# Five convolved tiles of the input projection as 512-column products, with VectorE joining the two halves

## The chip, the cores and the metric

The kernel runs on one core of one Trainium2 chip. The metric is the time of one execution on the device, in microseconds; three executions are shown below and their median is what counts. Engines are named as in the profile: PE is TensorE (PEld its weight loads), ACT is ScalarE, DVE is VectorE, SP issues the DMAs.

## The reference

One layer of a streaming encoder over 256 tokens. What matters here is the input projection `proj = rmsnorm(x) @ w_in` and what the second mixer does with 1280 of its columns (`xbc`):

```python
def causal_dwconv(x, w, b):
    k_w = w.shape[0]
    seq = x.shape[1]
    xp = jnp.pad(x, ((0, 0), (k_w - 1, 0), (0, 0)))
    return sum(xp[:, k:k + seq] * w[k] for k in range(k_w)) + b

def mamba2_mixer(p, conv_w, conv_b, dt_bias, a_log, d_skip, norm_g):
    ...
    xbc = jax.nn.silu(causal_dwconv(xbc, conv_w, conv_b))
    xs, b_in, c_in = jnp.split(xbc, [SSM_INNER, SSM_INNER + SSM_GROUPS * SSM_STATE], axis=-1)
```

All inputs are 32-bit floats.

## The kernel before

**Split products.** Each 32-bit matrix is used as two parts, `hi` (rounded to the format that PE multiplies fast) and `lo` (the rest). A product is the sum of three: hi·hi, hi·lo and lo·hi. Weights arrive as 1 MB tiles, numbered n through the whole kernel: SP loads tile n into `raw[n % 3]`, ACT casts it to `hi` (L400), DVE subtracts to get `lo` (L829), PE multiplies. The ring is three tiles deep (`RING = 3`), so SP may load tile n + 3 only after DVE has made `lo` of tile n. In round n of the loops ACT and DVE split tile n + 2.

**Two ways to multiply a tile of w_in.** A tile is 2048 x 128 weights; the activations have 256 tokens, and their two parts lie side by side in `ux` (`uh` and `ul` are its halves). `tile_product` (narrow) issues three 256-column matmuls for each of the 16 k-blocks, 48 in all (L1436, L1437, L1438), which add up all three products in the first 256 columns of a PSUM bank; it needs `lo` from the start. `wide_product` issues 16 matmuls of 512 columns with `hi` (L1461), which leave hi·uh in columns 0 to 255 and hi·ul in 256 to 511, and then 16 of 256 columns with `lo` (L1467) onto the first half. It needs `lo` only for its last third, but somebody has to add the halves. Tiles 8 to 13 and 25 to 33 are done wide: ACT copies the second half out (`take_low`, L517) and DVE adds the first (`sum_halves`, L958). Product banks go round by n % 3.

**The ten convolved tiles** are n = 15 to 24 (N_XBC = 15, N_QKV = 25), all narrow. In round n, ACT casts tile n + 2, waits for product n, then (`conv_first`) writes tap 0 with the bias to `convacc` (L590) and a copy of the product to `convraw` (L592), whose signal `tile_taken` also frees the bank; then it waits for DVE's `conv_done` of tile n - 1 and applies SiLU (L597, signal `xbc_ready`). DVE in round n makes `lo` of tile n + 2, does some small work that belongs to that round (the dt rows of the scan, variances, reciprocals, rotations), and then `conv_rest`: three taps, each a scalar_tensor_tensor that waits for the one before (L1055). `go` is the helper for an instruction after which DVE waits for its completion. Most buffers in SBUF appear in the profile under the one name `arena`.

**What follows.** Before tile 26 PE issues a few small matmuls (L1723, L1724) that need `xbc_ready` of all ten tiles. From round 27 on it spreads the decays of two heads of the scan each round (L1735, L1736), and for heads 2 and 3 it waits on `seg_ready`, which DVE signals at L1149 in its own round 27. Order is fixed by each engine's instruction list; nothing is scheduled at run time.

Of the kernel before, what the change touches and what calls it, by code (L numbers as in the profile page):

```python
# [17 lines left out]
ALU, ACT, AX = mybir.AluOpType, mybir.ActivationFunctionType, mybir.AxisListType  # L18

P = 128  # L20
T = 256
# [8 lines left out]
RING = 3  # L30
# [11 lines left out]
N_XK, N_XV, N_CQ, N_KRDT, N_XBC, N_QKV, N_ZA, N_U, N_ZB, N_OUT, N_WQ, N_WO, N_FFN = 0, 4, 8, 14, 15, 25, 31, 34, 38, 41, 57, 61, 65  # L42
# [6 lines left out]
V_CW = V_ROWS_A  # L49
# [42 lines left out]
def products(n):  # L92

    extra = {N_U: 3, N_U + 1: 3, N_U + 2: 6, N_U + 3: 1}
    return n + 1 + sum(v for m, v in extra.items() if m <= n)
# [25 lines left out]
def encoder(nc, x, mem, positions, norm_mix, w_in, mla_q_norm, mla_w_uq, mla_kv_norm, mla_w_ukv, mla_out_norm,  # L121
# [4 lines left out]
    with ctx:  # L126
        def sb(name, shape, dt=F32):
            return ctx.enter_context(nc.sbuf_tensor(name, shape, dt))
# [3 lines left out]
        def S(name):  # L132

            if name not in signals:
                signals[name] = Signal(ctx.enter_context(nc.semaphore(name)))
            return signals[name]
# [9 lines left out]
        vecs = sb("vecs", [P, V_ALL])  # L146
        small = sb("small", [P, 112])
        arena = sb("arena", [P, 20400])
        bank = [ctx.enter_context(nc.psum_tensor(f"bank{i}", [P, 512], F32)) for i in range(8)]
# [3 lines left out]
        def at(off, *shape):  # L153

            size = int(np.prod(shape))
            v = arena[:, off:off + size]
            if len(shape) == 2:
                v = v.rearrange("p (a b) -> p a b", b=shape[1])
            if len(shape) == 3:
                v = v.rearrange("p (a b c) -> p a b c", b=shape[1], c=shape[2])  # L160
            return v
# [9 lines left out]
        convraw, convacc = at(4096, RING, T), at(4864, RING, T)  # L171
# [219 lines left out]
        def _(act):  # L391
            a = Engine(act)
# [112 lines left out]
            def wait_product(n):  # L505
                act.wait_ge(S("products_done").sem, products(n))
# [71 lines left out]
            a.mark(act.copy(krT[64:128, :], b[0:64, 0:T]), S("kr_parts"))  # L578
            a.mark(act.copy(dt_rows[0:SSM_H, 0, :], b[64:64 + SSM_H, 0:T]), S("tile_taken"))
            act.wait_ge(S("tile_summed").sem, summed(N_CQ + 5))  # L580
            squares("cq", cq_raw[:, 0:4, :], sq_cq, 4)
            squares("ckv", cq_raw[:, 4:6, :], sq_ckv, 2)

            def conv_first(n):

                c = n - N_XBC
                wait_product(n)
                if c >= RING:
                    act.wait_ge(S("xbc_ready").sem, c - RING + 1)
                a.mark(act.activation(convacc[:, n % RING, :], bank[n % 3][:, 0:T], ACT.Identity,  # L590
                                      scale=vecs[:, V_CW + 30 + c:V_CW + 31 + c], bias=vecs[:, V_CB + c:V_CB + c + 1]), S("conv_first"))
                a.mark(act.copy(convraw[:, n % RING, :], bank[n % 3][:, 0:T]), S("tile_taken"))  # L592

            def conv_silu(n):
                c = n - N_XBC
# [218 lines left out]
        def _(dve):  # L814
# [3 lines left out]
            def go(ins, signal=None):  # L818
                d.mark(ins, signal or step)
                d.settle()  # L820
# [227 lines left out]
            def conv_rest(n):  # L1048

                c = n - N_XBC  # L1050
                dve.wait_ge(S("tile_taken").sem, TAKEN_XBC + c + 1)
                s = n % RING
                for k in (1, 2, 3):
                    col = V_CW + 10 * (3 - k) + c
                    go(dve.scalar_tensor_tensor(out=convacc[:, s, k:T], in0=convraw[:, s, 0:T - k], scalar=vecs[:, col:col + 1],  # L1055
                                                in1=convacc[:, s, k:T], op0=ALU.mult, op1=ALU.add),
                       S("conv_done") if k == 3 else None)

            def rotate(tile):

                for q in range(4):
                    d.mark(dve.tensor_copy(rot[32 * q:32 * q + 32, :], tile[32 * (q ^ 1):32 * (q ^ 1) + 32, :]), step)
                d.settle()
                go(dve.tensor_tensor(rot, rot, sinT, ALU.mult))
                go(dve.tensor_tensor(tile, tile, cosT, ALU.mult))
                go(dve.tensor_tensor(tile, tile, rot, ALU.add), S("rotated"))
# [5 lines left out]
            for n in range(N_XBC, N_XBC + 10):  # L1072
# [49 lines left out]
                if n == 23:  # L1122
                    feature_scale("cq", cq_raw[:, 0:4, :], 4, rtmp_a)
                conv_rest(n)
                if n == 24:
                    feature_scale("ckv", cq_raw[:, 4:6, :], 2, rtmp_b)
# [46 lines left out]
            for n in range(N_SSD, N_OUT + 1):  # L1173
# [27 lines left out]
                if N_U + 2 <= n <= N_ZB:  # L1201
                    k = n - N_U - 2
                    dve.wait_ge(S("tile_taken").sem, TAKEN_U + 7 + k)
                    rotate(qr[:, k, :])
# [218 lines left out]
        def _(pe):  # L1423
            done = S("products_done").sem

            def ready(n, i=None, per=0):

                pe.wait_ge(S("lo_ready").sem, n + 1 if i is None else i * per + n + 1)
# [11 lines left out]
            def tile_product(n, b, cols=P, mid=None, lo_signal=None, ks=(0, KD)):  # L1440

                s = n % RING
                for k in range(*ks):
                    if k == KD // 2 and mid:
                        mid()
                    if lo_signal and k % 2 == 0:
                        pe.wait_ge(S(lo_signal).sem, k + 2)
                    last = three(bank[b][0:cols, 0:T], hi[:, s, k * P:k * P + cols], lo[:, s, k * P:k * P + cols],
                                 uh[:, k, :], ul[:, k, :], k == 0, k == KD - 1)
                if ks[1] == KD:  # L1450
                    last.then_inc(done, 1)

            def wide_product(n, b, ks=(0, KD), i=None, mid=None, lo_signal=None):

                s = n % RING
                turn = 0 if i is None else i * GROUP
                pe.wait_ge(S("hi_ready").sem, turn + n + 1)
                for k in range(*ks):
                    if lo_signal and k % 2 == 0:
                        pe.wait_ge(S(lo_signal).sem, k + 2)  # L1460
                    pe.matmul(bank[b][:, :], hi[:, s, k * P:(k + 1) * P], ux[:, k, :, :].rearrange("p a b -> p (a b)"),  # L1461
                              start=(k == 0), stop=False)
                if mid:
                    mid()
                pe.wait_ge(S("lo_ready").sem, turn + n + 1)
                for k in range(*ks):
                    last = pe.matmul(bank[b][:, 0:T], lo[:, s, k * P:(k + 1) * P], uh[:, k, :], start=False, stop=(k == KD - 1))  # L1467
                if ks[1] == KD:
                    last.then_inc(done, 1)
# [116 lines left out]
            def both(f, pair):  # L1586
                f(2 * pair)
                f(2 * pair + 1)
# [93 lines left out]
            tile_product(N_KRDT, N_KRDT % 3, ROPE + SSM_H)  # L1682

            def w_in_tile(n, mid=None):
                if N_KRDT <= n - 3 < N_QKV:
                    pe.wait_ge(S("tile_taken").sem, TAKEN_XBC + n - 3 - N_KRDT)
                else:
                    pe.wait_ge(S("tile_summed").sem, summed(n - 3))
                if n < N_QKV:
                    ready(n)  # L1690
                    tile_product(n, n % 3, mid=mid)
                else:
                    wide_product(n, n % 3, mid=mid)
# [58 lines left out]
            def latent_tile(index, w0, wcols, k0, kn_, s):  # L1752
                if index < 3:
                    pe.wait_ge(S("tile_summed").sem, summed(N_ZA + index))
                else:
                    pe.wait_ge(S("tile_taken").sem, TAKEN_U + index - 2)
                b = bank[(products(N_U - 1) + index) % 3]
# [15 lines left out]
            for n in range(N_SSD, N_OUT):  # L1773
                s = n % RING
# [57 lines left out]
                else:  # L1832
                    pe.wait_ge(S("tile_taken").sem, TAKEN_U + 15 + (n - N_ZB) - 2)
                    wide_product(n, z_bank(n), mid=mid)
# [25 lines left out]
            for cb in range(4):  # L1860
                n = N_OUT + cb
# [6 lines left out]
            for cb in range(4):  # L1868
                n = N_OUT + 4 + 3 * cb
# [28 lines left out]
            for n in (N_WQ + 2, N_WQ + 3):  # L1898
                ready(n)

                def mid():
                    if n == N_WQ + 2:
                        pe.wait_ge(S("tile_taken").sem, TAKEN_U + 17)
                        both(scores, A_X // 2)
# [3 lines left out]
            both(head_out, A_X // 2)  # L1908
            pe.wait_ge(S("tile_taken").sem, TAKEN_U + 19)
            both(scores, A_X // 2 + 1)  # L1910
# [101 lines left out]
OUT_CHUNKS = [(3, cb) for cb in range(4)] + [(g, cb) for cb in range(4) for g in range(3)]  # L2012
N_VECTORS = 16 * (9 + 1 + 3 + 1)
TAKEN_XBC = 1
TAKEN_U = TAKEN_XBC + 10
N_SSD = 27
N_PAIR = 33


def summed(n):  # L2020

    return n - N_CQ + 1 - (11 if n > N_KRDT else 0) - (4 if n >= N_ZB else 0)


def z_bank(n):
    return n % 3 if n < N_U else (n - N_ZB + 1) % 3
# [58 lines left out]
```

## Time and profile before

| | us |
|---|---|
| median of 3 executions | 1180.62 |
| lowest, highest | 1179.78, 1180.98 |
| the profiled execution, whole | 1180.57 |
| its span, first to last instruction | 1178.4 |
| PE busy in it | 1165.5 (99%) |
| DVE busy | 898.6 (76%) |
| ACT busy | 660.3 (56%) |
| mean granted TensorE clock | 0.999 |

The w_in tiles begin at about 61 us; the feed-forward layer runs from about 450 us to the end. Times in the rows are microseconds from the span's start. "Busy" counts the time covered by an instruction's record, and consecutive matmuls overlap in the records, so the time of a tile is read from the start of its first matmul to the start of the next tile's first.

### The profile page before, as it was taken

The numbers are of one execution on the slowest core, as the hardware profiler recorded it, in microseconds if no ns is written. First come the engines' busy times: TensorE is split into PE (matmuls) and PEld (weight loads), VectorE is DVE, ScalarE is ACT, GpSimd is POOL, SyncE is SP. The second block draws the span as 40 slices with busy tenths as digits, with TensorE's granted clock in tenths as the row PEclk, the third lists the DMA queues.
The fourth block names the chain that finished last, engine by engine and source line by source line (L and its number), as shares of the span: only waits on it lengthen the run. The fifth ranks groups of instructions, "written<-read, shape, count | busy, mean of one in ns | idle before, by whom it ended". The sixth has DMA issues, their size and how long they took to land.

```text
span 1178.4 us, 18270 instructions
## 1 busy us (share of the span) xinstructions
PE 1165.5 (99%) x6666; PEld 1022.8 (87%) x6666; DVE 898.6 (76%) x1286; ACT 660.3 (56%) x872; POOL 3.0 (0%) x5
## 2 busy tenths in 40 slices
PE   8999999999999999999999999999999999999997
PEld 8889998898888988888888888888888888888885
DVE  6885998887966677777777776777777776777777
ACT  6646664566645567455555545455555545455455
POOL 0000000000000000000000000000000000000000
PEclk9999999999999999999999999999999999999999
DMA  9967646543666546675757566575757566575751
GB/s 346 261 153 191 180 129 164 154 119 110 223 205 183 195 127 175 181 212 179 214 178 203 179 190 191 164 213 178 214 178 202 179 192 187 166 213 178 214 179 71
DMA packets 303628, 217.00 MB, mean 184 GB/s; under 512 B 11383, under 2 KB 264543, under 8 KB 302943
## 3 DMA queue, kind: packets, MB, share of 16 engines
q1 hardware_dynamic: 303262, 215.91, 62.9%
q8 instruction: 30, 0.49, 0.2%
q10 hardware_dynamic: 320, 0.47, 0.1%
q14 instruction: 16, 0.12, 0.0%
HBM read 214.27 MB, written 2.10 MB: 184 GB/s over the span
## 4 chain that ended last, share of the span: by engine, by line
PE 92%; DVE 5%; issue 1%; ACT 1%; DMA 0%; DVEq 0%; ACTq 0%
PE bank L1461 32%; PE bank L1467 17%; PE bank L1433 10%; PE bank L1435 10%; PE bank L1434 10%; PE bank L1436 2%; PE bank L1614 2%; PE bank L1437 2%; PE bank L1438 2%; DVE lo L829 1%; PE bank L1552 1%; PE bank L1583 1%; DVE arena L1055 1%; PE bank L1490 1%; PE bank L1497 1%
## 5 line engine op out<-in xcount | busy, mean ns | idle before, releaser
L829 DVE TENSOR_TENSOR lo<-raw,hi 128x2048 fp32r<-128x2048 f32 x195 | 446.0, 2288 | 112.8 <-ACT hi L400 104.7
L400 ACT CAST hi<-raw 128x2048 fp32r<-128x2048 f32 x194 | 370.5, 1915 | 95.9 <-PE bank L1435 95.6
L1461 PE MATMUL bank<-ux,hi 128*128 128x512 f32 x1696 | 406.2, 391 | 0.0
L1461 PEld LDWEIGHTS bank<-ux,hi 128*128 128x128 f32 x1696 | 312.3, 188 | 61.2 <-DVE arena L1360 0.2
L1467 PEld LDWEIGHTS bank<-ux,lo 128*128 128x128 f32 x1696 | 217.2, 191 | 8.9 <-issue 1.0
L1467 PE MATMUL bank<-ux,lo 128*128 128x256 f32 x1696 | 221.2, 283 | 0.0
L1433 PE MATMUL bank<-hi,ch 128*128 128x512 f32 x462 | 180.7, 391 | 0.0
L1434 PE MATMUL bank<-lo,ch 128*128 128x512 f32 x462 | 179.5, 389 | 0.0
L1435 PE MATMUL bank<-hi,cl 128*128 128x512 f32 x462 | 179.5, 388 | 0.0
L783 ACT COPY arena<-bank 128x256 f32<-128x256 f32 x88 | 32.9, 374 | 195.1 <-PE bank L1467 195.0
L1339 DVE SCALAR_TENSOR_TENSOR arena<-arena,vecs 128x255 f32<-128x255 f32 (+1 forms) x176 | 85.0, 483 | 24.4 <-DVE arena L1339 3.6
L1435 PEld LDWEIGHTS bank<-hi,cl 128*128 128x128 f32 x462 | 86.7, 188 | 18.1
L1433 PEld LDWEIGHTS bank<-hi,ch 128*128 128x128 f32 x462 | 86.8, 188 | 17.5 <-issue 0.2
L1434 PEld LDWEIGHTS bank<-lo,ch 128*128 128x128 f32 x462 | 86.8, 188 | 17.2
L1359 DVE TENSOR_TENSOR arena<-bank,arena 128x256 f32<-128x256 f32 x88 | 37.1, 422 | 55.3 <-ACT arena L783 55.3
L1436 PE MATMUL bank<-ux,hi 128*128 128x256 f32 (+1 forms) x240 | 68.6, 286 | 0.0
L1438 PE MATMUL bank<-ux,lo 128*128 128x256 f32 (+1 forms) x240 | 67.8, 283 | 0.0
L1437 PE MATMUL bank<-ux,hi 128*128 128x256 f32 (+1 forms) x240 | 67.8, 283 | 0.0
L1272 DVE TENSOR_TENSOR arena<-arena,bank 128x512 f32<-128x512 f32 x96 | 60.9, 680 | 3.6 <-PE bank L1435 3.5
L771 ACT ACTIVATE arena<-arena,vecs 128x256 f32<-128x256 f32 x88 | 53.4, 607 | 17.2 <-DVE arena L1360 17.1
L1437 PEld LDWEIGHTS bank<-ux,hi 128*128 128x128 f32 (+1 forms) x240 | 45.3, 189 | 0.1
L1436 PEld LDWEIGHTS bank<-ux,hi 128*128 128x128 f32 (+1 forms) x240 | 45.3, 189 | 0.1
(274 smaller groups left out, 1014.9 us busy)
## 6 DMA issues: line engine op xcount, KB each, us to landing
raw<-in_ffn_w_up_dram SPq DMA_DIRECT2D x88, 1024.0 KB, 5.8
raw<-in_ffn_w_down_dram SPq DMA_DIRECT2D x44, 1024.0 KB, 5.1
raw<-in_w_in_dram SPq DMA_DIRECT2D x28, 1024.0 KB, 5.6
raw<-in_w_out_dram SPq DMA_DIRECT2D x16, 1024.0 KB, 5.3
raw<-in_cross_wkv_dram SPq DMA_DIRECT2D x7, 1024.0 KB, 10.0
arena<-in_x_dram SPq DMA_DIRECT2D x4, 1024.0 KB, 8.6
raw<-in_cross_wq_dram SPq DMA_DIRECT2D x4, 1024.0 KB, 5.5
raw<-in_cross_wo_dram SPq DMA_DIRECT2D x4, 1024.0 KB, 5.3
```

The costliest lines, as they stand in the source:

```text
L400: a.mark(act.copy(hi[:, n % RING, :], raw[:, n % RING, :]), S("hi_ready"))
L829: d.mark(dve.tensor_tensor(lo[:, n % RING, :], raw[:, n % RING, :], hi[:, n % RING, :].bitcast(F32), ALU.subtract), S("lo_ready"))
L1272: d.mark(dve.tensor_tensor(hres[:, t, cb * 512:(cb + 1) * 512], hres[:, t, cb * 512:(cb + 1) * 512], bank[b][:, :], ALU.add), signal)
L1339: go(dve.scalar_tensor_tensor(out=cacc[:, s, tap:T], in0=craw[:, s, 0:T - tap], scalar=vecs[:, bass.ds(col, 1)], in1=cacc[:, s, tap:T], op ...
L1433: pe.matmul(dst, xh, wh, start=start, stop=False)
L1434: pe.matmul(dst, xh, wl, start=False, stop=False)
L1435: return pe.matmul(dst, xl, wh, start=False, stop=stop)
L1436: pe.matmul(dst, wh, xh, start=start, stop=False)
L1437: pe.matmul(dst, wh, xl, start=False, stop=False)
L1438: return pe.matmul(dst, wl, xh, start=False, stop=stop)
L1461: pe.matmul(bank[b][:, :], hi[:, s, k * P:(k + 1) * P], ux[:, k, :, :].rearrange("p a b -> p (a b)"), start=(k == 0), stop=False)
L1467: last = pe.matmul(bank[b][:, 0:T], lo[:, s, k * P:(k + 1) * P], uh[:, k, :], start=False, stop=(k == KD - 1))
```

## The change

Tiles 15 to 19 (N_NARROW = N_XBC + 5 = 20) go through `wide_product` instead of `tile_product`. For them ACT's tap 0 takes columns 0 to 255 as before, and its copy takes columns 256 to 511. DVE gets two instructions ahead of its three taps: a scalar_tensor_tensor that adds tap 0 of the second half from PSUM to `convacc`, and a tensor_tensor that adds the first half from PSUM to the copy in `convraw`; the latter signals `tile_summed` and frees the bank. The counts of the signals follow.

```diff
@@ ACT, conv_first
-                a.mark(act.copy(convraw[:, n % RING, :], bank[n % 3][:, 0:T]), S("tile_taken"))
+                if n < N_NARROW:
+                    a.mark(act.copy(convraw[:, n % RING, :], bank[n % 3][:, T:2 * T]), S("low_taken"))
+                else:
+                    a.mark(act.copy(convraw[:, n % RING, :], bank[n % 3][:, 0:T]), S("tile_taken"))
@@ DVE, conv_rest
-                dve.wait_ge(S("tile_taken").sem, TAKEN_XBC + c + 1)
                 s = n % RING
+                if n < N_NARROW:
+                    dve.wait_ge(S("low_taken").sem, summed(n))
+                    go(dve.scalar_tensor_tensor(out=convacc[:, s, :], in0=bank[n % 3][:, T:2 * T], scalar=vecs[:, V_CW + 30 + c:V_CW + 31 + c],
+                                                in1=convacc[:, s, :], op0=ALU.mult, op1=ALU.add))
+                    go(dve.tensor_tensor(convraw[:, s, :], bank[n % 3][:, 0:T], convraw[:, s, :], ALU.add), S("tile_summed"))
+                else:
+                    dve.wait_ge(S("tile_taken").sem, TAKEN_XBC + n - N_NARROW + 1)
@@ PE, w_in_tile
-                if N_KRDT <= n - 3 < N_QKV:
-                    pe.wait_ge(S("tile_taken").sem, TAKEN_XBC + n - 3 - N_KRDT)
+                if n - 3 == N_KRDT:
+                    pe.wait_ge(S("tile_taken").sem, TAKEN_XBC)
+                elif N_NARROW <= n - 3 < N_QKV:
+                    pe.wait_ge(S("tile_taken").sem, TAKEN_XBC + n - 3 - N_NARROW + 1)
                 else:
                     pe.wait_ge(S("tile_summed").sem, summed(n - 3))
-                if n < N_QKV:
+                if N_NARROW <= n < N_QKV:
                     ready(n)
                     tile_product(n, n % 3, mid=mid)
@@ constants
+N_NARROW = N_XBC + 5
-TAKEN_U = TAKEN_XBC + 10
+TAKEN_U = TAKEN_XBC + N_QKV - N_NARROW
-    return n - N_CQ + 1 - (11 if n > N_KRDT else 0) - (4 if n >= N_ZB else 0)
+    return n - N_CQ + 1 - (1 if n > N_KRDT else 0) - (N_QKV - N_NARROW if n >= N_QKV else 0) - (4 if n >= N_ZB else 0)
```

In the lists below `arena` is SBUF (here `convacc` and `convraw`), `bank0` a PSUM bank, `vecs` the per-feature scalars, and the words after "waits" are the signals. DVE in round 15, before: the last two of the small instructions on the dt rows, the three taps of tile 15, and `lo` of tile 18.

```order
L1078 TENSOR_TENSOR arena<-arena 12x256 [waits vector_step]
L1079 TENSOR_SCALAR arena<-arena 12x256 [waits dt_abs]
L1055 SCALAR_TENSOR_TENSOR arena<-arena,vecs 128x255 [waits tile_taken,vector_step]
L1055 SCALAR_TENSOR_TENSOR arena<-arena,vecs 128x254 [waits vector_step]
L1055 SCALAR_TENSOR_TENSOR arena<-arena,vecs 128x253 [waits vector_step]
L829 TENSOR_TENSOR lo<-raw,hi 128x2048 [waits products_done,hi_ready,conv_done]
```

DVE at the same place in the changed kernel (its lines L1085 to L1088 are the old L1076 to L1079, L1064 is the old L1055, L832 the old L829):

```order
L1087 TENSOR_TENSOR arena<-arena 12x256 [waits vector_step]
L1088 TENSOR_SCALAR arena<-arena 12x256 [waits dt_abs]
L1057 SCALAR_TENSOR_TENSOR arena<-bank0,vecs,arena 128x256 [waits low_taken,vector_step]
L1059 TENSOR_TENSOR arena<-bank0,arena 128x256 [waits vector_step]
L1064 SCALAR_TENSOR_TENSOR arena<-arena,vecs 128x255 [waits tile_summed]
L1064 SCALAR_TENSOR_TENSOR arena<-arena,vecs 128x254 [waits vector_step]
L1064 SCALAR_TENSOR_TENSOR arena<-arena,vecs 128x253 [waits vector_step]
L832 TENSOR_TENSOR lo<-raw,hi 128x2048 [waits products_done,hi_ready,conv_done]
```

Two instructions stand ahead of the taps, each followed by a wait for its completion, and `lo` of tile 18 now stands behind five instead of three. The same is so in rounds 16 to 19.

PE from the end of tile 14 (76 columns of weights) into tile 15, before:

```order
L1437 MATMUL bank<-ux,hi 76x256
L1438 MATMUL bank<-ux,lo 76x256
L1436 MATMUL bank<-ux,hi 128x256 [waits lo_ready,tile_summed]
L1437 MATMUL bank<-ux,hi 128x256
L1438 MATMUL bank<-ux,lo 128x256
```

The same place in the changed kernel, with the whole of tile 15 and the first matmul of tile 16:

```order
L1446 MATMUL bank<-ux,hi 76x256
L1447 MATMUL bank<-ux,lo 76x256
L1470 MATMUL bank<-ux,hi 128x512 [waits hi_ready,tile_summed]
L1470 MATMUL bank<-ux,hi 128x512 x15
L1476 MATMUL bank<-ux,lo 128x256 [waits lo_ready]
L1476 MATMUL bank<-ux,lo 128x256 x15
L1470 MATMUL bank<-ux,hi 128x512 [waits hi_ready,tile_summed]
```

The three kinds of 256-column matmuls, 16 of each, have become 16 of 512 and 16 of 256 columns, and `lo` is waited for two thirds of a tile later.

## Rows read from the trace of the kernel before

**Rows 1.** The page: busy time of each engine, and DMA issues of w_in.

```profile
PE 1165.5 (99%) x6666; PEld 1022.8 (87%) x6666; DVE 898.6 (76%) x1286; ACT 660.3 (56%) x872; POOL 3.0 (0%) x5
...
raw<-in_w_in_dram SPq DMA_DIRECT2D x28, 1024.0 KB, 5.6
```

**Rows 2.** PE timeline: start us, us, engine, line, operation; first matmuls of tiles.

```profile
66.72 3.82 PE L1461 MATMUL bank<-ux,hi 128*128 128x512 f32 x16
...
72.29 3.82 PE L1461 MATMUL bank<-ux,hi 128*128 128x512 f32 x16
...
100.16 0.28 PE L1436 MATMUL bank<-ux,hi 128*128 128x256 f32 x1
...
105.91 0.28 PE L1436 MATMUL bank<-ux,hi 128*128 128x256 f32 x1
...
128.95 0.28 PE L1436 MATMUL bank<-ux,hi 128*128 128x256 f32 x1
```

**Rows 3.** DVE timeline in rounds 16 to 19; in brackets idle before, and releaser.

```profile
116.33 2.29 DVE L829 TENSOR_TENSOR lo<-raw,hi 128x2048 fp32r<-128x2048 f32 x1 [0.84 <-ACT hi L400]
...
123.25 2.29 DVE L829 TENSOR_TENSOR lo<-raw,hi 128x2048 fp32r<-128x2048 f32 x1
...
127.84 2.29 DVE L829 TENSOR_TENSOR lo<-raw,hi 128x2048 fp32r<-128x2048 f32 x1 [0.86 <-ACT hi L400]
...
130.04 0.41 DVE L1092 TENSOR_TENSOR arena<-arena 12x256 f32<-12x256 f32 x1
```

**Rows 4.** Windows, DVE alone: stretch, its length, DVE busy (instructions), clock, DMA.

```profile
127.90:179.50 51.60, 48.97 (x81) 1.00 0.60 159
```

**Rows 5.** The chain that ended last, from 123 to 181 us: start, length, what.

```profile
131.83 0.50 DVE arena L1055
132.35 0.49 DVE arena L1055
...
176.40 2.15 issue
180.24 0.38 PE bank L1735
```

**Rows 6.** Durations (min/median/max ns) by line, and DVE's timeline at 455 us.

```profile
L1164 DVE SCALAR_TENSOR_TENSOR arena<-arena,small,bank x6: 472/474/480, 189.4 to 223.1; 128x256 f32<-128x256 f32 x6
...
L958 DVE TENSOR_TENSOR arena<-bank,arena x18: 408/418/426, 67.6 to 288.5; 128x256 f32<-128x256 f32 x18
...
455.88 0.42 DVE L1359 TENSOR_TENSOR arena<-bank,arena 128x256 f32<-128x256 f32 x1
456.33 0.42 DVE L1360 TENSOR_TENSOR arena<-arena 128x256 f32<-128x256 f32 x1
```

**Rows 7.** Timeline of all engines around the two places where PE meets DVE's work.

```profile
165.49 0.42 ACT L597 ACTIVATE arena<-arena 128x256 f32<-128x256 f32 x1 [0.23 <-DVE arena L1055]
...
166.05 0.67 PE L1723 MATMUL bank<-arena 128*128 128x256 f32 x2
...
179.47 0.38 PE L1735 MATMUL bank<-acum_h,pick 128*128 128x256 f32 x1 [0.25 <-DVE arena L1149]
...
180.24 0.38 PE L1735 MATMUL bank<-acum_h,pick 128*128 128x256 f32 x1 [0.27 <-DVE arena L1149]
```

**Rows 8.** Waits of PE from 180 to 1170 us: total, times, longest.

```profile
PE bank L1562 <- issue: 0.7, 1, 0.7
PE bank L1735 <- DVE arena L1149: 0.3, 1, 0.3
```

**Rows 9.** PE's last matmul, and windows (length, PE busy, clock, DMA) behind it.

```profile
1169.61 0.39 PE L1435 MATMUL bank<-ux,cl 128*128 128x512 f32 x1
...
1174.00:1175.00 1.00, 0.00 (x0) 0.94 0.16 64
1175.00:1176.00 1.00, 0.00 (x0) 0.50 1.03 402
```

**Rows 10.** Waits of all engines from 90 to 200 us: total, times, longest.

```profile
ACT arena L590 <- PE bank L1438: 15.2, 9, 3.7
```

## The prediction, made before the changed kernel ran

> **What bounds the kernel now.** I read the page's busy times first: PE is busy for 99% of the span, DVE for 76% [rows 1], so at first sight only PE's own work counts, and a cheaper tile would be a gain. Then I asked PE's waits from 180 us to its end: two or three, about 1 us in all [rows 8]. So whatever PE loses before 180 us is not won back later, and whatever it gains before a wait is only worth something if the wait ends earlier too.
>
> The stretch that the change touches is 100 to 180 us, and there the chain of waits tells another story than the shares. From about 128 us on it runs through DVE and not through PE, one instruction behind the other, to the head spread at 180.24, which PE waits for [rows 5]. The reader should see two things. First, DVE is full: of the 51.6 us from 127.9 to 179.5 it is busy for 48.97, over 81 instructions [rows 4], and the 2.6 us that are left are the hand-over times of some 0.03 us between dependent instructions, not waits on another engine. Second, PE meets this chain at two places. At 166.05 it starts the small products that need all ten convolved tiles; the SiLU of the last one ran from 165.49 to 165.91, after a 0.23 us wait for DVE's taps [rows 7]. PE arrives there at the very moment when its operand is ready. At 179.47 and 180.24 it is already late, 0.25 and 0.27 us by the records, waiting for DVE's L1149 [rows 7]. So PE is full, and DVE is full behind it with no reserve: the two run neck and neck.
>
> **The change part by part.**
>
> PE's work. A wide tile takes 72.29 - 66.72 = 5.57 us, a narrow one 105.91 - 100.16 = 5.75 us [rows 2]. Five tiles at 0.18 make 0.9 us less of PE. This is the whole gain that the change can have.
>
> ACT's work. The same two instructions per tile with another address: nothing. ACT waits for PE 15.2 us in nine waits before tap 0 [rows 10], so its longer waits for `conv_done` have cover. I followed the one that could hurt: the SiLU of tile n - 1 stands ahead of the cast of tile n + 2. In round 18 the taps of tile 17 end at 125.3 (below), the SiLU and the cast of tile 21 take 0.4 and 1.9 us, and DVE needs that cast at 130.0. It is there 2.3 us earlier. If this cover went, DVE would be late by the difference.
>
> DVE's work. Two instructions more in each of five rounds. The scalar_tensor_tensor with a PSUM operand is L1164, 474 ns; the tensor_tensor is L958, 418 ns [rows 6]. Both are followed by a wait for completion. The taps show what that adds: 0.49 us each, but 132.35 - 131.83 = 0.52 from start to start [rows 5]; the PSUM add at 455.88 has a dependent instruction 0.45 behind it [rows 6]. So 0.51 + 0.45 = 0.96 us per round, 4.8 us in all. The bounds: if the hand-over were as short as the overlap that independent instructions get (`lo` at 127.84 lasts 2.29 us and the next instruction starts at 130.04 [rows 3], 0.09 before its end), 0.71 to 0.8 per round, 3.6 to 4.0 in all; above, nothing in the trace is dearer than the taps' 0.52, twice 0.52 makes 5.2.
>
> A rule against the rows: DVE's two PSUM rows are no dearer than their SBUF relatives (418 ns for L958 beside 0.42 us for L1360, which has no PSUM operand) [rows 6]. The Trainium skill, "VectorE: DVE Perf Modes", section on the TRN2 errata, has a fixed cost of 120 cycles for a PSUM source and 58 for SBUF at 0.96 GHz, some 65 ns more for each; by it ten instructions would cost 0.65 us more and the time would be 1184.3. The rows disagree, and I go by them.
>
> What of DVE's 4.8 us lies beside idle time. Between the first added instruction at about 109 us and the meeting at 179.5, DVE waits for another engine just twice: 0.84 us before 116.33 and 0.86 before 127.84, both for ACT's cast [rows 3]. After them it is gapless [rows 4]. Both are used up: by the first DVE is 1.9 us behind its old times, by the second 2.0 (1.9 - 0.84 + 0.96, and the fourth round's 0.96 on top). So DVE's delay is +1.0 in round 15, +1.9 in 16, less 0.84, +2.0 after 17, +3.0 after 18, less 0.86, +3.1 after 19, and stays there: 4.8 - 1.7 = 3.1 us.
>
> Who waits for that. (a) `lo` of tile 20, the first narrow one, which PE needs from its start: 123.25 + 2.0 + 2.2 = 127.5; PE comes to tile 20 at 128.95 - 0.9 = 128.0 [rows 2, 3]. It holds by 0.5 us; if it didn't, PE's wait would be covered by what follows. (b) Banks: the first half is now freed by DVE, not ACT, at the latest some 4 us before PE wants it for tile n + 3. (c) Loads: SP waits for `lo` to reload a raw buffer, a load lands after 5.6 us [rows 1] and ACT casts it about a round later than that; it is delayed alike with everything behind DVE, and at its tightest (tile 23, `lo` of tile 20 at 127.5, landed at 133.1, cast not before PE has done tile 20 at 133.8) it is in time. (d) The SiLU of tile 24: 165.49 + 3.1 = 168.6, so the small products at 169.1 instead of 166.05. (e) The spread of heads 2 and 3: 179.47 + 3.1.
>
> The sum. PE arrives at (d) at 166.05 - 0.9 = 165.1 and stands idle for 4.0 us, until 169.1. Its gain of 0.9 is swallowed there. The following 13 us of PE's work are the same as before, and at (e) DVE is again the later one, by 3.1. From there both go on as before, PE without waits that could absorb anything [rows 8]. The change is +3.1 us on the profiled execution of 1180.57, which is 0.05 below the median: **1183.7 us**, 0.26% slower.
>
> **The rivals.**
>
> *PE sets the end and the gain arrives.* The shares speak for it (99% against 76%), and that PE before 166 has no waits. Then the change is -0.9 and the time 1179.7, not slower. It is one mechanism at one place: the small products at 166.05. It decides this way if the ten added instructions delay the last SiLU by no more than what DVE's idle time swallows, 1.7 us, thus under 0.35 us per round instead of 0.96. Against it is the length of each of the two, 418 and 474 ns.
>
> *Cheap hand-overs.* At 0.8 us per round the delay is 4.0 - 1.7 = 2.3 us, the time 1182.9; at 0.71 it is 1182.4. For it: some DVE pairs overlap. Against it: both new instructions have a wait behind them in the list.
>
> *The clock falls in PE's new idle time.* At the end of this trace PE's last matmul ends at 1170.0, and the granted clock goes from full to half at about 1174.9 (0.94 in that microsecond, 0.50 after) [rows 9], 4.9 us after PE stopped; the new pause is 4.0 us long. If it fell there, PE would start again at half speed. For a spell as long as the pause it would lose 2.0 us, of which about 0.4 are covered before the wait at (e), since PE arrives there early by that much: +1.6, 1185.3. The Trainium skill, "TensorE: Matmul & The Clock Gate", advises against idle gaps of PE about this long and would put the clock at 1.2 GHz for a while; the end of this trace agrees that it falls, though only after a longer stop.
>
> *The change does not do what it says* (a tile still goes narrow, or PE waits for `lo` at the start of a wide one): the order shows 16 and 16 matmuls with `lo_ready` in the middle, so I give it nothing.
>
> **How the numbers follow.** My forecast (DVE's delay of about 3.1) 0.77, with 1183.0 to 1184.4 as its own range; the clock 0.11; cheap hand-overs 0.07; the gain arrives 0.05. A measurement of this kernel can tell about 0.2% from no change, 2.4 us, so slower means above 1183.0. Forecast and clock are above, the two others below it; some of the forecast's lower edge may fall under, so slower 0.84, same 0.15, faster 0.01 (it would need 1178.2, more than the whole gain). The range takes in cheap hand-overs and the clock: 1182.4 to 1185.4.
>
> **What would show it.** Right: tiles 15 to 19 at 5.57 us from start to start; DVE's two new lines at about 0.47 and 0.42, and no wait for ACT's cast left between 110 and 175; one pause of PE of about 4 us before the small products, released by the SiLU; the wait for L1149 at about 182.6 as short as before; everything after at +3.1. Wrong: PE pausing earlier (tile 20), or ACT's cast still keeping DVE waiting, which would mean a longer way through ACT; a wide tile in this place slower than 5.57; a pause much shorter than 4 us, which would mean that DVE had reserve that the rows don't show; a granted clock under 1.00 behind the pause.

## The result: 1183.5 us, 2.8 slower than before

| | before | changed |
|---|---|---|
| median of 9 executions, us | 1180.66 | 1183.48 |
| lowest, highest | 1179.65, 1181.47 | 1183.03, 1184.92 |
| ratio, 95% interval | | 1.0029 (1.0019 to 1.0038) |
| span of the profiled execution | 1178.4 | 1181.6 |
| DVE busy | 898.6 | 903.5 |
| mean granted TensorE clock | 0.999 | 0.996 |

The forecast was 1183.7, in a range of 1182.4 to 1185.4. The page of the changed kernel: PE is busy as long as before and DVE 4.9 us longer [rows 1]; in the chain that ended last, DVE's share has gone up to 7% (from 5%).

```profile
PE 1165.8 (99%) x6586; PEld 1020.0 (86%) x6586; DVE 903.5 (76%) x1296; ACT 658.9 (56%) x872; POOL 3.0 (0%) x5
...
PE 91%; DVE 7%; issue 1%; ACT 1%; DMA 0%; DVEq 0%; ACTq 0%
```

PE's timeline (start, length, line, operation, and in brackets idle time and releaser) answers to [rows 2] and [rows 7]. L1470 and L1476 are the old L1461 and L1467, L1734 the small products (L1723), L1746 the spreads (L1735):

```profile
105.36 3.82 PE L1470 MATMUL bank<-ux,hi 128*128 128x512 f32 x16
...
110.92 3.82 PE L1470 MATMUL bank<-ux,hi 128*128 128x512 f32 x16
...
162.79 2.07 PE L1476 MATMUL bank<-ux,lo 128*128 128x256 f32 x16
168.93 1.19 PE L1734 MATMUL bank<-arena 128*128 128x256 f32 x2 [4.06 <-ACT arena L600]
...
171.48 4.11 PE L1470 MATMUL bank<-ux,hi 128*128 128x512 f32 x16
...
183.37 0.28 PE L1746 MATMUL bank<-acum_h,pick 128*128 128x256 f32 x1
```

The wide tiles take 110.92 - 105.36 = 5.56 us. PE is done with tile 25 at 164.9 and stands idle for 4.06 us, until ACT's SiLU (L600, the old L597) has the last convolved tile. DVE's timeline answers to [rows 3] and [rows 6]; L832 is `lo`, L1064 the taps:

```profile
108.42 0.48 DVE L1057 SCALAR_TENSOR_TENSOR arena<-bank,vecs,arena 128x256 f32<-128x256 f32 x1
108.94 0.42 DVE L1059 TENSOR_TENSOR arena<-bank,arena 128x256 f32<-128x256 f32 x1
109.40 1.52 DVE L1064 SCALAR_TENSOR_TENSOR arena<-arena,vecs 128x255 f32<-128x255 f32 x3
110.95 2.29 DVE L832 TENSOR_TENSOR lo<-raw,hi 128x2048 fp32r<-128x2048 f32 x1
...
117.08 2.29 DVE L832 TENSOR_TENSOR lo<-raw,hi 128x2048 fp32r<-128x2048 f32 x1
...
129.73 2.29 DVE L832 TENSOR_TENSOR lo<-raw,hi 128x2048 fp32r<-128x2048 f32 x1
```

The pair takes 109.40 - 108.42 = 0.98 us, and the two brackets of [rows 3], 0.84 and 0.86 us of waiting for ACT's cast, are gone at 117.08 and 129.73.

**How executions are compared below.** PE's start of tile 14, before anything that was changed, lies anywhere from 94.17 (this profile) over 94.56 (before) to 95.99 us in the profiled executions. So places in the traces are given from that start: the small products ("first meeting") and the start of tile 28, behind the spread of heads 2 and 3 ("second meeting").

| | tile 14 at | small products, from there | tile 28, from there | median, us | its before | ratio (95%) |
|---|---|---|---|---|---|---|
| before | 94.56 | 71.49 | 86.02 | 1180.66 | | |
| changed | 94.17 | +3.27 | +3.64 | 1183.48 | 1180.66 | 1.0029 (1.0019 to 1.0038) |
| no_adds | 94.56 | -0.74 | -0.73 | 1179.70 | 1180.44 | 0.9992 (0.9983 to 1.0001) |
| load_only | 95.12 | +3.27 | +3.72 | 1184.10 | 1180.44 | 1.0027 (1.0017 to 1.0036) |
| load_in_gap | 95.11 | +0.01 | +0.02 | 1179.84 | 1180.44 | 0.9996 (0.9987 to 1.0005) |
| pe_kept_busy | 95.79 | +3.26 | +3.28 | 1183.20 | 1180.44 | 1.0023 (1.0014 to 1.0032) |
| two_wide | 95.03 | +0.32 | +0.32 | 1180.77 | 1180.38 | 1.0001 (0.9992 to 1.0011) |
| gap_filled_0 | 94.55 | -0.02 | -1.17 | 1179.37 | 1180.38 | 0.9990 (0.9981 to 1.0000) |
| gap_filled_2 | 95.39 | -0.38 | -1.53 | 1179.32 | 1180.71 | 0.9987 (0.9978 to 0.9996) |
| gap_filled_3 | 95.99 | -0.57 | -1.72 | 1178.38 | 1180.71 | 0.9982 (0.9973 to 0.9991) |
| gap_filled_4 | 95.19 | -0.26 | -1.13 | 1179.99 | 1180.38 | 0.9996 (0.9987 to 1.0005) |
| gap_filled_5 | 95.74 | +0.68 | -0.18 | 1179.92 | 1180.38 | 0.9998 (0.9989 to 1.0007) |
| ten_wide | 94.57 | +8.15 | +9.11 | 1189.24 | 1180.71 | 1.0073 (1.0059 to 1.0086) |

### The profile page after: what moved, and what is told of

Same layout as the page of the kernel before. It is cut to its first block, busy times and chain, and to the rows that moved or that the text cites. A ratio compares the mean times of both kernels' runs of the same rounds, so it can differ in the third digit from the quotient of the medians.

```text
span 1181.6 us, 18120 instructions
## 1 busy us (share of the span) xinstructions
PE 1165.8 (99%) x6586; PEld 1020.0 (86%) x6586; DVE 903.5 (76%) x1296; ACT 658.9 (56%) x872; POOL 3.0 (0%) x5
## 4 chain that ended last, share of the span: by engine, by line
PE 91%; DVE 7%; issue 1%; ACT 1%; DMA 0%; DVEq 0%; ACTq 0%
PE bank L1470 32%; PE bank L1476 17%; PE bank L1442 10%; PE bank L1443 10%; PE bank L1444 10%; PE bank L1623 2%; DVE lo L832 2%; PE bank L1445 1%; PE bank L1446 1%; PE bank L1447 1%; DVE arena L1064 1%; PE bank L1561 1%; PE bank L1592 1%; PE bank L1499 1%; PE bank L1506 1%
## 5 line engine op out<-in xcount | busy, mean ns | idle before, releaser
L832 DVE TENSOR_TENSOR lo<-raw,hi 128x2048 fp32r<-128x2048 f32 x195 | 446.1, 2288 | 110.0 <-ACT hi L400 101.8
L1470 PE MATMUL bank<-ux,hi 128*128 128x512 f32 x1776 | 425.4, 391 | 0.0
L1470 PEld LDWEIGHTS bank<-ux,hi 128*128 128x128 f32 x1776 | 327.2, 188 | 64.1 <-DVE arena L1369 0.2
L1476 PEld LDWEIGHTS bank<-ux,lo 128*128 128x128 f32 x1776 | 227.5, 191 | 9.3 <-issue 1.0
L1476 PE MATMUL bank<-ux,lo 128*128 128x256 f32 x1776 | 231.6, 283 | 0.0
L1445 PE MATMUL bank<-ux,hi 128*128 128x256 f32 (+1 forms) x160 | 46.0, 287 | 0.0
L1446 PE MATMUL bank<-ux,hi 128*128 128x256 f32 (+1 forms) x160 | 45.2, 282 | 0.0
L1447 PE MATMUL bank<-ux,lo 128*128 128x256 f32 (+1 forms) x160 | 45.2, 282 | 0.0
L1369 DVE TENSOR_TENSOR arena<-arena 128x256 f32<-128x256 f32 x88 | 37.4, 426 | 3.0
L882 DVE SCALAR_TENSOR_TENSOR ux<-bank,vecs,ux 128x256 fp32r<-128x256 f32 x64 | 26.6, 476 | 14.6 <-ACT ux L456 14.6
```

The costliest lines, as they stand in the source:

```text
L832: d.mark(dve.tensor_tensor(lo[:, n % RING, :], raw[:, n % RING, :], hi[:, n % RING, :].bitcast(F32), ALU.subtract), S("lo_ready"))
L1445: pe.matmul(dst, wh, xh, start=start, stop=False)
L1446: pe.matmul(dst, wh, xl, start=False, stop=False)
L1447: return pe.matmul(dst, wl, xh, start=False, stop=stop)
```

## The experiments

Theory A is the forecast's: DVE's queue says when PE may go on at both meetings. Theory B: PE's own work sets the end. Theory C: the wide form itself costs, in ACT or in the banks.

### DVE's load without the wide products, and the wide products without DVE's load

load_only: the kernel before, with

```diff
@@ conv_rest, all ten tiles narrow
+                if n < N_XBC + 5:
+                    go(dve.scalar_tensor_tensor(out=dec[:, 0, 0:T], in0=bank[5][:, T:2 * T], scalar=vecs[:, V_CW + 30:V_CW + 31],
+                                                in1=convacc[:, s, :], op0=ALU.mult, op1=ALU.add))
+                    go(dve.tensor_tensor(dec[:, 1, 0:T], bank[5][:, 0:T], convraw[:, s, :], ALU.add))
```

> The kernel before (all ten tiles narrow), with two DVE instructions of the same size and kind added ahead of the taps in rounds 15 to 19; they read an idle PSUM bank and write to an unused place, so the result is untouched. Theory A: DVE is late by 5 x 0.98 - 1.64 = 3.3 us at the small products and at the head spread; PE, which has no cheaper tiles, waits 2.9 us there instead of 4.0. The end moves by about 3.2, 1183.5 to 1183.9, although no product has changed. Theory C: 1180.7.

```profile
169.88 1.19 PE L1738 MATMUL bank<-arena 128*128 128x256 f32 x2 [3.12 <-ACT arena L600]
...
172.43 4.18 PE L1474 MATMUL bank<-ux,hi 128*128 128x512 f32 x16
```

That is PE's timeline at the small products. They start 169.88 - 95.12 = 74.76 us behind tile 14; in the changed kernel it is 168.93 - 94.17 = 74.76. With narrow tiles and ten DVE instructions whose results nobody reads, PE resumes at the same hundredth, only from a pause of 3.12 instead of 4.06 us (2.9 was expected). So the delay is DVE's load and nothing else, and the cheaper products don't shorten it at all: they lengthen the pause. Theory C is out. The median, 1184.10, is 0.2 above the range that was expected, much less than the width of its interval (2.0 to 4.2 us over the kernel before).

no_adds: the changed kernel with

```diff
@@ conv_rest
-                    go(dve.scalar_tensor_tensor(out=convacc[:, s, :], in0=bank[n % 3][:, T:2 * T], scalar=vecs[:, V_CW + 30 + c:V_CW + 31 + c],
-                                                in1=convacc[:, s, :], op0=ALU.mult, op1=ALU.add))
-                    go(dve.tensor_tensor(convraw[:, s, :], bank[n % 3][:, 0:T], convraw[:, s, :], ALU.add), S("tile_summed"))
...
-                       S("conv_done") if k == 3 else None)
+                       S("conv_done") if k == 3 else S("tile_summed") if k == 1 and n < N_NARROW else None)
```

> The changed kernel, with DVE's two new instructions left out: the second half's share of tap 0 and the first half of the product are missing from the five tiles; everything else, the wide products too, stays. Theory A (DVE's queue sets when PE may go on at both meeting points): DVE is back at its old times, PE reaches the small products 0.9 us early and waits for the same SiLU as before, so the time is that of the kernel before, 1180.7. Theory B (PE sets the end, the gain of the products is real and only the adds hide it): 0.9 us less, 1179.8. Theory C (the loss is made by the wide form itself: the hand-over of banks, ACT's copy): 1183.5 as changed.

Here theory A as I had put it missed and B had the number: 0.74 us less at both meetings, and 0.74 in the medians (the interval just includes no change). Two lines of DVE's timeline tell why:

```profile
115.95 2.29 DVE L832 TENSOR_TENSOR lo<-raw,hi 128x2048 fp32r<-128x2048 f32 x1 [0.47 <-ACT hi L400]
...
127.09 2.29 DVE L832 TENSOR_TENSOR lo<-raw,hi 128x2048 fp32r<-128x2048 f32 x1 [0.48 <-ACT hi L400]
```

In [rows 3] these stand at 116.33 and 127.84, with 0.84 and 0.86 of waiting. What DVE waits for is ACT's cast, which is queued behind ACT's waits for PE's products. When PE's tiles get shorter the casts come earlier and DVE with them, by 0.38 and 0.75. DVE's old times were not its own: up to 127.84 PE set them, through ACT; behind that DVE runs on its own and carries the lead of 0.75 to both meetings. So PE's gain does reach the end once nothing is added to DVE, 0.74 of the 0.9. The other 0.2 is a short wait of PE at the first meeting: the `lo` part of tile 25 starts 0.94 us earlier than before (163.18 against 164.12), and the small products 2.13 us behind it, where 1.91 pass when PE waits for nothing (gap_filled_3 below). In that much theory A holds: DVE still says when PE may go on.

### The same load where DVE is idle

load_in_gap: ten such instructions, in a row behind `split(N_KRDT + 2)`, ahead of the 5.9 us in which DVE waits for the cast of tile 17.

> The kernel before, with the same ten DVE instructions, all of them placed where DVE sits idle for 5.9 us ahead of the lo part of tile 17. Theory A: 4.9 us of work in a gap of 5.9, so nothing moves, 1180.7. If added DVE work costs wherever it stands (ports, contention with PE or ACT): toward 1183.5.

DVE's wait ahead of `lo` of tile 17, in the kernel before and in this run:

```profile
105.15 2.29 DVE L829 TENSOR_TENSOR lo<-raw,hi 128x2048 fp32r<-128x2048 f32 x1 [5.89 <-ACT hi L400]
```

```profile
105.75 2.29 DVE L832 TENSOR_TENSOR lo<-raw,hi 128x2048 fp32r<-128x2048 f32 x1 [1.16 <-ACT hi L400]
```

The ten instructions have filled the gap (5.89 us of waiting have become 1.16), and counted from tile 14 `lo` of tile 17 starts where it did (10.64 us behind it instead of 10.59). Nothing moved: +0.01 and +0.02 in the trace, and the median 0.6 below its before, inside the interval. The instructions are harmless here; in the full stretch they are not.

### Two tiles, ten tiles

two_wide and ten_wide are the changed kernel with `N_NARROW = N_XBC + 2` and `N_XBC + 10`.

> The change for tiles 15 and 16 only. Theory A: two rounds add 1.96 us to DVE, its two idle stretches swallow 1.64, so DVE is 0.3 late: 1181.0. If the cost goes by the number of wide tiles: two fifths of 2.8, 1181.8. If PE's gain counted: 1180.3.

> The change carried on to all ten convolved tiles, nothing moved. Theory A: in rounds 20 to 24 DVE has no idle time at all, so each further wide tile costs its full 0.98 us; 3.27 + 4.9 = 8.2 us of delay at the small products, 1188.6, and up to 1 more for the clock, which falls in PE's longer pause. If each wide tile costs alike (2.8 / 5 = 0.57): 1186.2.

Two tiles cost 0.32 at both meetings (expected 0.3), ten cost 8.15 at the first (expected 8.2). Per tile that is 0.16 and 0.82: the price of a wide tile depends on how much idle time is left for it. The whole curve is one line, 0.98 a round less 1.63 us. The 1.63 was taken from the five tiles (3.27); two and ten, for which the line gives 0.33 and 8.17, are its test. At the second meeting the ten cost 9.11: there the clock adds 0.96 (next section). The medians (+0.39 and +8.5) agree within their intervals.

### The clock in the pause

Windows of PE in the changed kernel (stretch, length, busy and instructions, granted clock, DMA share, GB/s):

```profile
167.00:168.00 1.00, 0.00 (x0) 1.00 0.00 0
168.00:169.00 1.00, 0.07 (x1) 0.76 0.66 148
169.00:170.00 1.00, 1.00 (x3) 0.50 1.14 345
171.00:172.00 1.00, 1.00 (x4) 0.53 1.10 264
172.00:173.00 1.00, 1.00 (x6) 1.00 0.00 1
```

The clock goes to half at 168.5, just before PE resumes, and comes back at 171.95. The small products take 2.55 us (168.93 to 171.48) where they took 1.30 before, and tile 26 with its two spreads 6.32 instead of 6.13: 1.44 us lost at the lower level. pe_kept_busy fills the pause:

```diff
@@ PE, n == 26, ahead of the wait for xbc_ready
+                    for _ in range(14):
+                        pe.matmul(bank[7][:, :], ux[:, 0, 0, 0:P], ux[:, 0, :, :].rearrange("p a b -> p (a b)"), start=True, stop=True)
```

> The changed kernel, with 14 more 512-column matmuls (3.2 us) on data that is there, into a bank that the next product overwrites, in PE's 4.06 us pause before the small products. The granted clock should stay at 1.00 where it fell to 0.50 from 168.5 to 172.0. Theory: the fall cost what is left after PE's reserve at the next meeting, 0.4 us in the typical run and 1.5 in the two that took 1184.7 and 1184.9; so 1183.1, with no run over 1183.9. Rival: the fall costs all that the slower instructions show, 1.4 us, 1182.1. Rival: it costs nothing, 1183.5.

```profile
170.54 0.67 PE L1736 MATMUL bank<-arena 128*128 128x256 f32 x2 [0.86 <-ACT arena L600]
...
183.97 0.38 PE L1748 MATMUL bank<-acum_h,pick 128*128 128x256 f32 x1 [0.28 <-DVE arena L1158]
...
184.74 0.39 PE L1748 MATMUL bank<-acum_h,pick 128*128 128x256 f32 x1 [0.27 <-DVE arena L1158]
```

The granted clock stays at 1.00 through the pause. The small products start at the same place (+3.26), now at full speed, and PE is early enough at the second meeting to wait for DVE's L1158 (the old L1149) again, with the same two brackets as in [rows 7]. Tile 28 comes at +3.28 instead of +3.64: the fall cost 0.36 us in the profiled execution, the 1.44 less some 1.1 that PE would have waited anyway. That reserve can be read by itself: from the start of tile 27's `lo` part to tile 28 the kernel before takes 180.58 - 177.14 = 3.44 us, the changed one 183.83 - 181.46 = 2.37, so it was 1.07. It holds for the other two falls too: in load_only 1.51 us are lost and the second meeting is 0.45 later than the first, in ten_wide 2.02 and 0.96, so 1.06 are hidden in each. The medians (1183.20 against 1183.48, from different comparisons) are too close to show it. The second half of the expectation missed: three executions still took 1184.6 to 1184.7, at a clock of 0.998 or 0.999. One of them is the profiled one, whose tile 14 starts 1.6 us later than the changed kernel's. At least that one is late from its beginning, not from the clock.

### DVE's other work moved into the gap

gap_filled_k: k tiles wide, and ahead of `split` of tile 17

```diff
+            for wide_ in (pick, acum_h, acum_l):
+                d.mark(dve.memset(wide_[:, :].bitcast(F32), 0.0), step)
+            d.mark(dve.memset(krT_odd[0:64, :], 0.0), step)
+            for g in range(2):
+                d.mark(dve.memset(swa_key[g][0][64:128, :], 0.0), step)
+            dve.wait_ge(S("tile_taken").sem, TAKEN_XBC)
+            go(dve.tensor_scalar(r0, r0, row12[:, 0:1], None, ALU.add))
...
+            sum_tiles("cq", sq_cq, 4, sum_cq)
+            sum_tiles("ckv", sq_ckv, 2, sum_ckv)
```

with the same lines taken out of rounds 15, 16, 21, 22 and 24, and with them a wait for completion behind the three in round 21.

> All ten tiles narrow, as before, but 4.5 us of DVE's small work is moved up into its 5.9 us gap ahead of the lo part of tile 17: the clearing of three small buffers and of three halves of key buffers, the four instructions on the dt rows, and the sums of squares. Theory A: DVE is early enough at the small products (where PE waits for nothing now) and at the head spread, where PE lost 1.07 us before; so 1179.6. Theory B (PE alone sets the end): 1180.7.

With no wide tile the first meeting is where it was and the second 1.17 us earlier: PE's old stall there is gone (expected 1.07). So the moved work is worth 1.17 us by itself, without any cheaper product. The median, 1179.37 (expected 1179.6), has an interval that just reaches no change.

> The change as it was made (tiles 15 to 19 wide), with the same work moved into the gap. Theory A: DVE's delay at the small products is 3.3 - 3.8 = -0.6 us, PE would come 0.9 early, so it waits 0.3 or so; at the head spread some 0.7; the time is 1179.4, 4 us below the changed kernel although every instruction of the change is there. Theory C (the wide form itself): 1183.5 less 1.07.

> The same moves, and tiles 15 to 18 wide. DVE gets 3.9 us of adds and has 1.6 us of waits plus 3.8 to 4.5 us of moved work to set against them, so PE's 0.72 us of cheaper tiles should arrive on top of the 1.07: 1178.9. If any other limit stands close behind DVE (ACT's casts): 1179.6 or more.

Both came out short of the expectation: 1179.92 and 1179.99, and in the traces -0.18 and -1.13 instead of -1.3 and -1.8. DVE's timeline of gap_filled_0 shows the error:

```profile
105.14 2.29 DVE L832 TENSOR_TENSOR lo<-raw,hi 128x2048 fp32r<-128x2048 f32 x1 [0.67 <-ACT hi L400]
...
112.72 1.52 DVE L1064 SCALAR_TENSOR_TENSOR arena<-arena,vecs 128x255 f32<-128x255 f32 x3 [1.54 <-ACT arena L595]
116.31 2.29 DVE L832 TENSOR_TENSOR lo<-raw,hi 128x2048 fp32r<-128x2048 f32 x1 [2.06 <-ACT hi L400]
...
127.83 2.29 DVE L832 TENSOR_TENSOR lo<-raw,hi 128x2048 fp32r<-128x2048 f32 x1 [0.87 <-ACT hi L400]
```

The 2.8 us taken out of rounds 15 and 16 have turned into waits of 1.54 and 2.06 in round 16, and `lo` of tile 21 starts at 127.83 as it did at 127.84. Work moved ahead of a wait is worth no more than the wait lets through: rounds 15 and 16 can take their two adds (1.96 us) for nothing, rounds 17 and 18 have 0.87 against their 1.96, round 19 has nothing. The sum was redone from this. With the 1.0 us cleared out of rounds 21 and 22, and casts that come some 0.4 earlier by round 18, five wide tiles give DVE 1.09 + 0.98 - 1.0 - 0.4 = +0.7 at the first meeting (trace +0.68), and four give -0.3 (trace -0.26), where PE alone would be at -0.9 and -0.7. This was worked out with the results of those two runs at hand; its test is the next two, by which three wide tiles should fit:

> DVE's small work moved into its gap, and tiles 15 to 17 wide. With four wide tiles PE still waited 0.34 us at the small products and about 0.3 at the head spread; one round less takes 0.98 us off DVE and 0.18 off PE's gain. So no wait at either place, and all of 3 x 0.18 + 1.07 = 1.6 us: 1178.8. If the DVE queue is not the reason of those waits, the time falls by the lost gain only: 1180.0.

> The same with tiles 15 and 16 wide: 2 x 0.18 + 1.07 = 1.4 us, 1179.0. Together with 0, 3, 4 and 5 wide tiles it shows where the best number lies: theory A has it at 3.

```profile
166.91 0.59 PE L1731 MATMUL bank<-arena 128*128 128x256 f32 x2
...
179.82 0.28 PE L1743 MATMUL bank<-acum_h,pick 128*128 128x256 f32 x1
...
180.29 2.01 PE L1467 MATMUL bank<-ux,hi 128*128 128x512 f32 x8
```

In gap_filled_3 PE waits at neither meeting: no bracket at the small products (L1731) nor at the spread (L1743). It is at -0.57 and -1.72, the full 3 x 0.18 + 1.17, of which the three wide tiles make 0.55 and the moved work the rest. Its median, 1178.38 us, is the lowest of all, with a ratio of 0.9982 (0.9973 to 0.9991) to the kernel before. Two wide tiles give 1179.32 and 0.9987 (0.9978 to 0.9996), an interval that excludes no change as well. In the traces three are 0.19 us better than two, as expected; the intervals of the medians are too wide to tell the two apart.

## Why the prediction was right, and where it was off

**What bounds it: right.** That DVE is full from 127.9 on and that PE meets it at two places [rows 4, 5, 7] decided the sign. load_only showed it.

**PE's gain of 0.9: right in size, and as forecast it never arrived.** From tile 14 to tile 20 PE takes 127.62 - 94.17 = 33.45 us where it took 128.95 - 94.56 = 34.39: 0.94 less.

**DVE's load: 0.96 us per round forecast, 0.98 measured.** The new lines in the changed kernel, from 106 to 180 us (group, count, busy us, mean ns):

```profile
L1064 DVE SCALAR_TENSOR_TENSOR arena<-arena,vecs 128x255 f32<-128x255 f32 (+2 forms) x30 | 14.5, 483 | 1.0
L1057 DVE SCALAR_TENSOR_TENSOR arena<-bank,vecs,arena 128x256 f32<-128x256 f32 x5 | 2.4, 481 | 0.1
L1059 DVE TENSOR_TENSOR arena<-bank,arena 128x256 f32<-128x256 f32 x5 | 2.1, 424 | 0.2
```

L1057 took 481 ns, not the 474 of L1164, and each pair has the hand-over of the taps. The one that reads PSUM is no dearer than the taps from SBUF (481 beside 483). The Trainium skill ("VectorE: DVE Perf Modes", section on the TRN2 errata) would have it some 65 ns dearer, an estimate from its 120 and 58 cycles at 0.96 GHz; by these rows it is not so here.

**Idle time swallowed: 1.70 forecast, 1.63 measured** (5 x 0.98 - 3.27). DVE's delay at the first meeting: 3.1 forecast, 3.27 in the trace.

**The time: nearer than the mechanism, by luck.** "Everything after at +3.1" was the forecast; counted from tile 14 it is +3.64 at the second meeting and still +3.61 at PE's last matmul (1172.83, before 1169.61). The sum was short by 0.17 of DVE's load and by 0.36 of the clock. The median moved by only 2.8, with an interval of 2.2 to 4.5 us from the ratio, which holds both numbers. That it lies 0.2 from the forecast and not 0.6 comes from parts of the execution that the change doesn't touch, as far as the profiled one shows: its tile 14 began 0.39 us earlier than in the kernel before.

**Waits behind it: right.** No wait of PE before the small products (`lo` of tile 20 held), none of DVE on ACT in the covered part; the pause was 4.06 us where 4.0 was forecast, and its releaser the SiLU. One sign did not show: the wait for the old L1149 at the second meeting was to stay as short as before, and it is gone, since PE came there late after the fall of the clock.

**The rival "PE sets the end" was priced wrongly.** Its point of decision was put at 1.7 us of added work in all. no_adds shows what I had overlooked: the two waits that swallow the load are themselves waits for PE, by way of ACT. The gain pulls their ends forward, and with nothing added 0.74 of it arrives. For the change itself this made no difference, since five adds overrun both waits.

**The clock: wrong.** The likeliest case held that it stays, with 0.11 for the fall, and named a granted clock under 1.00 behind the pause as a sign against itself. It fell, in the profiled execution and, by their mean clocks of 0.995 or 0.996, in eight of the nine (the ninth has 0.997, which some executions without a long pause have too). What kept the forecast near was the cover: 1.44 us lost at the lower level, of which the second meeting hid some 1.1. I had put the loss at 2.0, with a spell at half speed as long as the pause, for which no row spoke: PE worked at the lower level for 3.0 us and lost about half of that. And I had put the reserve at 0.4, where the two waits of [rows 7] together came to 1.07. The rival's +1.6 was therefore too dear: it is 0.36.

## What to carry to other kernels

An engine at 99% is not alone in deciding if another one is full over the stretch at hand: read the busy time per stretch, and follow the chain to the places where the two meet. Saving 0.18 us on the one for 0.98 us on the other pays only where the second has idle time that nothing downstream needs, and that idle time has a place: work put ahead of a wait is free up to the wait's length and gains nothing beyond it. Before adding to an engine's queue, move what can be moved out of it; here that, with three wide tiles for five, turned a loss of 3.6 us in the trace into a gain of 1.7 (2.8 and 2.3 by the medians), of which the moving alone gives 1.17.

## What the runs showed of the hardware

The granted clock went to half in pauses of PE shorter than the 4.9 us at the end of the trace of before [rows 9]: at 168.5 in the changed kernel, 3.6 us after PE's last matmul, and at 169.6 in load_only, 2.8 us after it, in a pause of 3.12 us:

```profile
168.00:169.00 1.00, 0.00 (x0) 1.00 0.00 0
169.00:170.00 1.00, 0.12 (x1) 0.79 0.81 143
```

In both a transfer begins in the same microsecond (the DMA share goes from 0.00 to 0.66 and 0.81), so one might suspect it. In ten_wide the clock falls 3.5 us after the last matmul, in a pause of 9.51 us, with no transfer under way:

```profile
168.00:169.00 1.00, 0.00 (x0) 0.58 0.00 0
```

It stayed at full in the profiled pauses of 1.48 us (gap_filled_5) and 0.86 us (pe_kept_busy). In load_only seven of ten executions have a mean clock of 0.995 or 0.996, one has 0.997, and two have 0.998 and 0.999, as executions without a long pause have; so by the means it fell in some and not in others, with a pause of about 3 us. The Trainium skill ("TensorE: Matmul & The Clock Gate", section on HAM oscillation) warns of idle gaps of PE about this long; the traces agree, and load_only's 3.12 us is a little shorter than the gap that section names. The half level is the lower of the clock's two, 1.2 GHz. The clock was back at full 3.0 us after PE had resumed in the changed kernel, 3.1 in load_only, and 4.2 in ten_wide.
